# First expert pass's rows by products with a 0/1 matrix, third pass's by a gather of whole rows; modulation rows loaded at two times

## The reference, cut to what matters

```python
for i in range(DEPTH_2):                       # the two attention blocks
    mod = c_act @ w_ada[i] + b_ada[i]          # six rows of 1024: the modulation rows
    sh1, sc1, g1, sh2, sc2, g2 = [m[:, None, :] for m in jnp.split(mod, 6, axis=-1)]
    h = rmsnorm(x, mix_norm[i]) * (1.0 + sc1) + sh1
    ...
    x = x + g1 * y
    h = rmsnorm(x, ffn_norm[i]) * (1.0 + sc2) + sh2
    x = x + g2 * hier_moe(h, ...)

# an MoE: route each token to a group, then to two experts of that group
a = jnp.einsum('td,edf->tef', t, w_gate)
u = jnp.einsum('td,edf->tef', t, w_up)
hidden = jax.nn.silu(a) * u * combine[..., None].astype(t.dtype)
out = jnp.einsum('tef,efd->td', hidden, w_down)
```

## Time and profile before

| | |
|---|---|
| median of 3 runs | 2014.77 us (2012.82 to 2016.58) |
| the profiled execution | 2019.38 us, of which its span is 2017.6 |
| PE busy | 1926.7 us, 95% of the span |
| DVE busy | 951.1 us, 47% |
| ACT, POOL busy | 435.5 us (22%), 326.8 us (16%) |
| mean granted PE clock | 0.979 of full speed |

### The profile page before, as it was taken

One profiled execution on the slowest core, in us unless ns is written; L12 is line 12 of the kernel. 1 busy time (PEld: TensorE's weight loads), 2 busy tenths in 40 slices (PEclk: granted clock), 3 DMA queues, 4 the chain that ended last, 5 costly groups with the idle time before them and its releaser, 6 DMA issues. The chain is left out here.

```text
span 2017.6 us, 20813 instructions
## 1 busy us (share of the span) xinstructions
PE 1926.7 (95%) x7482; PEld 1022.3 (51%) x7482; DVE 951.1 (47%) x1803; ACT 435.5 (22%) x1051; POOL 326.8 (16%) x548
## 2 busy tenths in 40 slices
PE   8999999999999999999799998999997999999995
PEld 4444444558885444543345445545433656645441
DVE  3443734547776022633363555535334367625333
ACT  1111101013333100110151105511001546612000
POOL 1000000000002000133010006502332003301333
PEclk9999999999999999999898999999997999999997
DMA  5222373730003125599844782137996202046996
GB/s 193 102 104 103 137 257 114 255 137 1 1 1 124 45 103 196 198 345 391 335 154 146 273 331 85 56 153 274 351 412 259 70 24 84 2 169 247 331 406 248
DMA packets 123401, 363.87 MB, mean 180 GB/s; under 512 B 26572, under 2 KB 31976, under 8 KB 110752
## 3 DMA queue, kind: packets, MB, share of 16 engines
q1 hardware_dynamic: 83200, 196.16, 27.0%
q10 hardware_dynamic: 26064, 133.70, 16.9%
q0 software_dynamic: 14032, 32.64, 4.6%
HBM read 335.07 MB, written 39.88 MB: 186 GB/s over the span
## 5 line engine op out<-in xcount | busy, mean ns | idle before, releaser
L447 PE MATMUL bank<-featT,ring 128*128 128x512 f32 x384 | 170.4, 597 | 3.0 <-DMA ring<-in_w_in 3.0
L2583 PE MATMUL bank<-ring,featT 128*128 128x512 f32 x384 | 168.9, 601 | 2.2 <-DVE small L2675 1.6
L1416 PE MATMUL bank<-ring,work 128*128 128x512 f32 x384 | 166.5, 593 | 3.0 <-PEq L1198 1.0
L1708 PE MATMUL bank<-work 128*128 128x512 f32 x384 | 168.8, 592 | 0.0
L2076 POOL DMA_INDIRECT work<-x_rows,small x132 | 131.7, 998 | 218.4 <-DVE work L2040 155.4
L2583 PEld LDWEIGHTS bank<-ring,featT 128*128 128x128 f32 x384 | 73.5, 193 | 93.4 <-issue 91.6
L1416 PEld LDWEIGHTS bank<-ring,work 128*128 128x128 f32 x384 | 72.2, 190 | 91.2 <-issue 91.2
L1732 DVE TENSOR_TENSOR work<-work,bank 128x256 f32<-128x256 f32 x39 | 16.5, 422 | 213.9 <-ACT work L1729 213.8
L447 PEld LDWEIGHTS bank<-featT,ring 128*128 128x128 f32 x384 | 71.8, 192 | 85.0 <-issue 81.9
L1708 PEld LDWEIGHTS bank<-work 128*128 128x128 f32 x384 | 71.1, 190 | 80.4 <-issue 80.4
L546 PE MATMUL bank<-ring,featT 128*128 128x512 f32 x256 | 110.4, 593 | 0.9 <-PEq L427 0.9
(11 more groups left out here) (507 smaller groups left out, 3067.2 us busy)
## 6 DMA issues: line engine op xcount, KB each, us to landing
ring<-in_w_in SPq DMA_DIRECT2D x15, 2048.0 KB, 11.6
ring_halves<-in_w_ada SPq DMA_DIRECT2D x48, 512.0 KB, 6.5
y_rows<-work ACTq DMA_DIRECT2D x39, 512.0 KB, 11.6
state<-in_w_ada SPq DMA_DIRECT2D x24, 512.0 KB, 6.8
ada_w<-in_w_ada SPq DMA_DIRECT2D x24, 512.0 KB, 6.5
ring<-in_fox_w_in SPq DMA_DIRECT2D x6, 2048.0 KB, 11.7
work<-in_moe_w_gate ACTq DMA_DIRECT2D x12, 1024.0 KB, 7.2
work<-in_moe_w_up ACTq DMA_DIRECT2D x12, 1024.0 KB, 10.4
```

The costliest lines, as they stand in the source:

```text
L447: last = nc.tensor.matmul(bank[b % 4][:, :], w[:, k, (b % 4) * P:(b % 4 + 1) * P], featT[:, k, :], start=(k == 0), stop=(k == KD - 1))
L1416: last = nc.tensor.matmul(bank[j % 4][:, :], outT[:, k, t * P:(t + 1) * P], w[:, k, :], start=(k == 0), stop=(k == KD - 1))
L1708: last = nc.tensor.matmul(gu_sum[par][at], xgT[par][:, k, at], w_gu[place_of[u]][:, k, :, :], start=(k == 0), stop=(k == KD - 1))
L2583: last = nc.tensor.matmul(f_bank(j)[:, :], featT[:, k, t * P:(t + 1) * P], w[:, k, :], start=(k == 0), stop=(k == KD - 1))
```

## The change

1. Pass 0's x is no longer gathered and transposed. PE multiplies the tokens' rows, which still lie on chip, by a 0/1 matrix of tokens by slots (`first_rows`, 32 products of 128x128), and gets them in feature order.
2. Pass 2 joins pass 1 in having a list of whole rows (N_WHOLE = 3); PE makes the two lists in `next_lists` (8 products with one column). Its x is turned by PE instead of DVE.
3. `pick` shrinks from 5 links to 4: the compare is on ranks for three experts. `slots` and `expert` move from the first block into the second, with pass 0's `keep_x_dve` and the copy of the lists in their midst. `pass_slots` and `parts` move into pass 0's `gate_up`, ahead of its fifth and seventh eighth.
4. Modulation rows 4 and 5 (and the layer-norm rows of `late`) are loaded after the `down` product of pass 4, rows 0 to 3 after the `gate_up` of pass 10, with no wait for the last expert's weights. `add_bias` is done on six parts of 1024: one each in passes 9 and 10, three in pass 11, one in pass 12.

```diff
-        N_WHOLE, NQ = 2, 4
+        N_WHOLE, NQ = 3, 4
...
+        def modulation_loads(sp, l, after_fifth, places_free):
+            for i in range(6):
+                sp.dma_start(b_row(i), D["b_ada_2"][l:l + 1, i * DM:(i + 1) * DM]).then_inc(first_rows_landed, 16)
...
+            after_fifth()
+            for i in (4, 5):
+                sp.dma_start(ada_sum[:, i * DM:(i + 1) * DM], ada_part[l, :, i * DM:(i + 1) * DM]).then_inc(first_rows_landed, 16)
             places_free()
-            for i in range(6):
+            for i in range(4):
                 load(sp, ada_sum[:, i * DM:(i + 1) * DM], ada_part[l, :, i * DM:(i + 1) * DM])
...
-            BIAS_AT = {NP - 2: (0, 1), NP - 1: (2, 3)}
+            BIAS_AT = {NP - 4: (4,), NP - 3: (5,), NP - 2: (0, 1, 2), NP - 1: (3,)}
...
                     PE.done(last, "ranks")
-                    keep_clock(2)
-                    for a in range(2 * T):
-                        if a in (0, T):
-                            DV.wait(pe, ("pick", N_PICK - 2 + a // T))
-                        last = nc.tensor.matmul(bank[6][:, P:P + N_WHOLE], slot_is[:, a * P:(a + 1) * P], tok_of[:, a * N_WHOLE:(a + 1) * N_WHOLE], start=(a == 0), stop=(a == 2 * T - 1))
-                    PE.done(last, "slots")
-                    keep_clock(4)
+                    keep_clock(1)
...
-                def gate_up(e, par):
+                def gate_up(e, par, between={}):
                     for k in range(KD):
+                        if k in between:
+                            between[k]()
...
+                    def first_rows():
+                        DV.wait(pe, ("pick", 1))
+                        for k in range(KD):
+                            for t in tiles:
+                                last = nc.tensor.matmul(bank[k // 4][:, (k % 4) * P:(k % 4 + 1) * P], eighth(x_tok[:, t, :], k), is_listed[0][:, t * P:(t + 1) * P],
+                                                        start=(t == 0), stop=(t == T - 1))
+                        last.then_inc(M_xT.sem, 1)
+
+                    def next_lists():
+                        for i in range(1, N_WHOLE):
+                            DV.wait(pe, ("pick", 1 + i))
+                            for t in tiles:
+                                last = nc.tensor.matmul(bank[6][:, P + i - 1:P + i], is_listed[i][:, t * P:(t + 1) * P], tok_id[:, t:t + 1], start=(t == 0), stop=(t == T - 1))
+                        PE.done(last, "slots")
...
-                        gate_up(e, par)
+                        gate_up(e, par, {4: pass_slots, 6: parts} if e == 0 else {})
                         if e + 1 < N_WHOLE:
-                            turn_x(pe, e + 1, 1 - par, 0)
+                            turn_x(pe, e + 1, 1 - par, (e + 1) // 2)
...
-                    keep_clock(1)
-                    pass_slots()
-                    keep_clock(1)
-                    turn_x(pe, 0, 0, 0)
-                    parts()
+                    first_rows()
+                    next_lists()
                     keep_clock(1)
...
-                        def places_free():
-                            sp.wait_ge(M_gu.sem, v(M_gu, pass_of[users[3][-1]]))
-                            wait_gate_up(sp, NE - 1)
-                        modulation_loads(sp, mod, places_free)
-                    if late:
-                        late(sp)
+                        def after_fifth():
+                            sp.wait_ge(M_down.sem, v(M_down, pass_of[users[4][-1]]))
+                            if late:
+                                late(sp)
+                        modulation_loads(sp, mod, after_fifth, lambda: sp.wait_ge(M_gu.sem, v(M_gu, pass_of[users[3][-1]])))
...
+                    slots_and_experts()
                     slots_of_passes()
                     rows_of_tokens()
                     weights_of_tokens()
```

More of the change, by code:

```diff
@@ L1598, in _ @@
                     link(V.tensor_tensor(by_two(is_at), bcast(place.unsqueeze(2), P, N_SORTED, N_SORTED), bcast(e_idx[:, 0:N_SORTED].unsqueeze(1), P, N_SORTED, N_SORTED), ALU.is_equal))
-                    PE.wait(dve, "slots")
-                    DV.done(V.tensor_copy(slot_tok, bank[6][:, P:P + N_WHOLE]), "slot_tok")
-                    link = chain(DV, dve, "slots")
-                    link(V.tensor_tensor(by_two(above), by_two(is_at), bcast(at_row.unsqueeze(1), P, N_SORTED, N_SORTED), ALU.mult))
@@ L1604, in _ @@
-                    link(V.reduce_sum(base[:, N_FIXED:NE], by_two(above), X_AXIS))
-                    link(V.tensor_scalar(room[:, N_FIXED:NE], place, len(FULL) - 0.5, float(HALF_SLOTS), ALU.is_lt, ALU.mult))
-                    link(V.tensor_tensor(t16(rowf), t16(ranks), bcast(base.unsqueeze(1), P, T, NE), ALU.add))
-                    link(V.scalar_tensor_tensor(out=t16(over), in0=t16(ranks), scalar=float(HALF_SLOTS), in1=bcast(room.unsqueeze(1), P, T, NE), op0=ALU.subtract, op1=ALU.is_ge))
@@ L1608, in _ @@
-                    link(V.scalar_tensor_tensor(out=kept_row, in0=over, scalar=FAR, in1=rowf, op0=ALU.mult, op1=ALU.add))
-                    link(V.tensor_tensor(two(prod2), two(O12), bcast(kept_row.unsqueeze(1), P, 2, T * NE), ALU.mult))
-                    link(V.reduce_sum(row_in, prod2.rearrange("p (a n) -> p a n", n=NE), X_AXIS))
-                    link(V.tensor_scalar(row_pass, row_in, 1.0 / P, 0.5 - 0.5 / P, ALU.mult, ALU.subtract))
-                    link(V.tensor_scalar(row_pass, row_pass, WHOLE, WHOLE, ALU.add, ALU.subtract))
@@ L1613, in _ @@
-                    link(V.scalar_tensor_tensor(out=slot_in, in0=row_pass, scalar=-float(P), in1=row_in, op0=ALU.mult, op1=ALU.add))
-                    link(V.tensor_tensor(in_pass.rearrange("p (a q) -> p a q", q=NP), bcast(row_pass.unsqueeze(2), P, 2 * T, NP), bcast(e_idx[:, 0:NP].unsqueeze(1), P, 2 * T, NP), ALU.is_equal))
-                    link(V.tensor_tensor(four(tok_in), four(in_pass), bcast(tok_far.unsqueeze(1).unsqueeze(3), P, 2, T, NP), ALU.mult))
-                    for i in range(2):
-                        link(V.tensor_tensor(by_slot[:, i], bcast(iota.unsqueeze(1), P, T, P), bcast(slot_in[:, i * T:(i + 1) * T].unsqueeze(2), P, T, P), ALU.is_equal))
@@ L2043, in add_bias @@
                     def add_bias(i):
-                        part = ada_sum[32 * i:32 * i + 1, i * B_ADA:(i + 1) * B_ADA]
-                        dve.wait_ge(loaded, mod_loads)
-                        DV.done(nc.vector.tensor_tensor(part, part, b_ada[32 * i:32 * i + 1, :], ALU.add), ("bias", i))
+                        p = 32 * (i % 4)
+                        part = ada_sum[p:p + 1, i * DM:(i + 1) * DM]
+                        if i < 4:
+                            dve.wait_ge(loaded, mod_loads)
+                        else:
+                            dve.wait_ge(first_rows_landed, 16 * 8 * (mod + 1))
+                        DV.done(nc.vector.tensor_tensor(part, part, b_row(i), ALU.add), ("bias", i))
                     def body(e):
```

77 lines of the change are left out of this document (49 added, 28 removed).

## The result

The changed kernel takes **2061.84 us** (median of four runs, 2060.01 to 2063.64), the kernel before 2014.67 beside it (2012.82 to 2016.58): a ratio of **1.0234, 95% interval 1.0216 to 1.0252**. The forecast was 2022.1, in a range of 2011 to 2031: the side is right, the size is not. So the traces differ by 41.7 us where the medians differ by 47.

A forecast was written before the change was run, and what follows sets the result against it. PE was taken as the bound, busy 1926.7 of 2017.6 us. Routing 18.6, pass 2's turn 2.7, clock 6.9, ends -11.3 and -8.2, row sums -1.4 gave +7.3 on 2014.8: 2022.1 us, range 2011 to 2031.

The forecast's parts named there:

- the price of `first_rows`: Routing of each MoE: 64 records at 0.112 us take 7.2 us; 7.8 as the slower bound.
- the routing: From the ranks to pass 1's `gate_up`: 6.2 us later per MoE, +18.6 us for three.
- the uncovered chain: DVE's 7.9 us of small operations after `parts` lose pass 0's `gate_up` as cover; PE stands some 6 us per MoE.
- The clock's +6.9: After each new 6 us wait, the next PE work runs at a lowered clock: 2.3 us per MoE, +6.9 in all.
- the clock holds: Rival: a 6 us wait leaves the clock up, the 6.9 falls away; -1.0 in all, 2013.8 us; chance 0.15.
- quick-product rivals: `first_rows` at 3.6 us: -3.5 in all, 2011.3 us, chance 0.06; at 5.4 us: +1.9, 2016.7 us, chance 0.08.
- Pass 2's turn, +2.7: PE's 8 more transposes between pass 1's `gate_up` and the following `down`: 0.9 us per MoE, +2.7 for three.
- The ends, -11.3 and -8.2: Ends of the first and second MoE: earlier modulation rows remove PE's pass-12 wait for `times_up`, saving 11.3 and 8.2 us.
- DVE is ready for the adds at 980.1: First MoE's end: DVE adds three biases until 983.6, before pass 12's `gate_up` ends at 985.07, so `times_up` isn't held up.
- the earlier loads hold up the weights: Rival: rows sent at 963.75 delay the last expert's weights, some 3 us in each of two MoEs; +13, 2028 us; chance 0.12.
- the prediction's own signs of being wrong: Pass 0's `times_up` directly behind `silu`, `first_rows` under 5 us, PE waiting for weights' DMA, or DVE waiting in pass 11 for rows.
- The row sums, -1.4: PE's 12 records behind the second MoE took 8.08 us against 5.3; half of a possible 2.8 us gain taken.

The follow-up runs named there:

- run 1: The changed kernel with `first_rows` reading 128 neighbouring columns instead of every eighth (wrong features in the first pass): 2029.22 us, ratio 1.0057 to the kernel before.
- run 5: The changed kernel with `first_rows` reading every second column (first MoE), every fourth (second), or with operands exchanged (third): 2049.03 us, a single execution.
- run 9: The changed kernel with the turns of the second and third pass's columns done as products with the identity instead of transpositions: 2068.18 us, a single execution.
- Run 2: The changed kernel with DVE's 7.9 us chain on tokens' rows and weights put behind pass 0's `gate_up` and pass 1's x copy: 2041.33 us, ratio 1.0117.
- run 3: The kernel before, old routing kept, with the changed kernel's two times of loading modulation rows and its spread biases: 2004.96 us, ratio 0.9945.
- run 6: Run 3's kernel, but the four later modulation rows wait again for the last expert's weights: 2004.70 us, ratio 0.9945.
- run 7: Run 3's kernel, with the next block's first 2 MB of weights issued only when the eleventh pass's y is kept: 2001.43 us, ratio 0.9937.
- run 10: The changed kernel with the next block's first 2 MB of weights issued only when the eleventh pass's y is kept: 2058.73 us, ratio 1.0209.
- run 8: The changed kernel with the edits of run 1 and Run 2 together (wrong features): 2009.13 us, ratio 0.9970.

## Why the prediction was wrong

**The step that failed** is the price of `first_rows`: "The delta-net's products of that shape, each with a stationary operand of its own, follow each other by 0.45 us per four records, 0.112 each: 7.2 us", with 7.8 as its upper bound. Shape and count were right; how the operand lies in memory was not looked at. The delta-net's operands are neighbouring columns, `first_rows` reads every eighth. It measured 15.50: +8.3 in each MoE, 25 of the 27 us by which the routing missed. (The slow rows behind it add 3.5, and the old routing's longer second MoE takes 2.2 off.) Runs 1, 5 and 9 show the cause. The only reads of every eighth column by PE in the trace of before were the turns, 1.05 us for eight, transpositions, which don't show it: a row of the same shape, or of the same access, is not yet a row of the same operation with the same access.

**The mechanism of the uncovered chain was right.** PE waits 5.96 us behind pass 0's `gate_up`, three times; the forecast was "some 6 us". Run 2 removed it and 20.5 us with it, clock included.

**The clock's +6.9 was right.** Pass 1's `gate_up` took 9.49 us in the first MoE against 7.10 before, and in the three together 7.2 us more. Run 2 gave it back. That the clock would fall ahead of the wait too, in pass 0's `gate_up`, was not forecast. The rival "the clock holds" falls, and so do both quick-product rivals.

**Pass 2's turn, +2.7**, is as forecast: 1.05 us each.

**The ends, -11.3 and -8.2, were too high.** They measured -5.4 and -6.7, and a further 1.2 us lost at pass 12's weights in the first MoE stands in the passes' line. The rows themselves were in time, as forecast: no bias waits for them. The step that failed here is "DVE is ready for the adds at 980.1", ahead of the end of pass 12's `gate_up`: in the changed kernel DVE can go on only at 1009.80, 2.9 us behind that end. What was left out is who else waits when the DMA engines are full. The rival "the earlier loads hold up the weights" named the last expert's weights, and that took place, as one of the prediction's own signs of being wrong, at 1.2 to 2.3 us, in the first MoE alone, instead of 3 in each of two. The larger part came by a third reader that no rival named: ACT's stores of y, whose buffers DVE must fill again before it comes to `keep_h`. Runs 3, 6, 7 and 10 show this. That engines take turns between queues is what the Trainium skill says ("DMA: Bandwidth & Descriptors", Queues, rings and completion order); the runs agree as far as 2 MB less on SP's queue shortened the wait for a store on ACT's by 3.9 us in runs 7 and 10, where 2 MB at 410 GB/s are 5.1.

**The row sums, -1.4,** measured -1.0, against the 8.08 us of the earlier trace rows:

```profile
1564.97 7.08 PE L2206 MATMUL bank<-work,ones 128*128 128x512 f32 x12 [3.12 <-PEq L1399]
```

The other -2.8 of the table's last line weren't taken apart: -3.4 lie between the first MoE's sums and the second's ranks, but ahead of the first ranks the two traces differ by +1.3 already.

Together: routing +26.6, passes +1.7, ends and the rest +6, on a forecast of +7.3, make the 41.7 of the traces. Without the strided read, run 1's 13.4 us over the kernel before would have been 6 above the forecast's 7.3.

## What to carry to other kernels

Price a product by a row with the same operation **and** the same access pattern on both operands: here 4-byte elements 16 bytes apart or more doubled each record of a product, while a transposition with the same read wasn't slowed. When a load is moved earlier in a stretch where the DMA engines are already full, ask which store or load it pushes back and who stands behind that one in program order; then move what nobody needs yet behind it, not the load that is needed. And when a long step is moved ahead, look which small operations lose their cover: putting 7.9 us of them behind pass 0 gave 20 us back.

## What the runs showed of the hardware

The granted clock can fall without idle time of PE in the profile ahead of it. In the strided products weight loads fill the whole window above at a clock of 1.00 and PE has no gap, yet what follows is slow: the changed kernel's first eight records of pass 0's `gate_up` took 5.11, 3.60 and 5.60 us in its three MoEs. This window of the second run lies over such a row; its granted clock of 0.55 of 2.4 GHz says that most of it lies at 1.2 GHz:

```profile
860.00:865.00 5.00, 5.00 (x8) 2.05 (x7) 1.43 (x4) 0.48 (x1) 1.71 (x2) 0.55 0.66 181
```

With a step of one these records took 3.60 us in all six MoEs of runs 1 and 8; with a step of eight they varied from 3.60 to 5.76. That is part of the rest of run 1's gain, 32.6 against the 24.3 that 8.1 us less in each `first_rows` would give. Why the fall comes in some MoEs and not in others stays open.

Why a transposition isn't slowed by the strided read stays open too; the runs only show that it isn't.
